# Level masks of a blockwise triangular inverse: from the matrix on GpSimd to the first product's copy on VectorE

## The reference, cut to what matters

```
a_mat = jnp.where(strict, jnp.einsum('bhnik,bhnjk->bhnij', kb, k) * decay, 0.0)
rhs = jnp.concatenate([v * beta[..., None], kb * jnp.exp(gc)[..., None]], axis=-1)
sol = lax.linalg.triangular_solve(a_mat + jnp.eye(CHUNK, dtype=jnp.float32), rhs,
                                  left_side=True, lower=True, unit_diagonal=True)
```

## Time and profile before

| what | value |
| --- | --- |
| median of 3 runs, lowest, highest | 2103.43, 2102.64, 2104.16 us |
| profiled execution: its time, its span | 2101.1 us, 2099.4 us |
| TensorE matmul, busy share of the span | 84% |
| VectorE, ScalarE, GpSimd | 62%, 46%, 10% |
| mixer, first layer | from 291 to some 547 us |
| mixer, second layer | from 1332 to some 1578 us |
| mean granted TensorE clock | 0.923 of full speed |

### The profile page before, as it was taken

How to read it: one execution, slowest core, us unless ns; L and a number is a source line. 1 busy time by engine, 2 the same in 40 slices (tenths; PEclk the granted TensorE clock), 3 DMA queues, 4 the chain that set the end, 5 groups by cost and what they waited for, 6 DMA issues and landing times. The chain is left out here.

```text
span 2099.4 us, 38037 instructions
## 1 busy us (share of the span) xinstructions
PE 1760.4 (84%) x14245; PEld 1412.2 (67%) x14246; DVE 1294.8 (62%) x1877; ACT 958.4 (46%) x1486; POOL 211.8 (10%) x267
## 2 busy tenths in 40 slices
PE   5499978999698399999954999899987939999991
PEld 0299767888444188888843997788873538888881
DVE  0439635666443488696646495576662469999664
ACT  0134533343311288686633445343332238888641
POOL 0000022222000000000010000222220010000002
PEclk8699999999798599999986999999997969999995
DMA  9532043000557499798833220000004069999744
GB/s 393 238 110 79 5 147 128 3 2 2 172 218 274 192 387 399 283 392 339 300 144 111 87 83 1 13 12 2 3 2 143 31 228 389 407 397 397 311 171 180
DMA packets 96326, 376.48 MB, mean 179 GB/s; under 512 B 14478, under 2 KB 35030, under 8 KB 65478
## 3 DMA queue, kind: packets, MB, share of 16 engines
q1 hardware_dynamic: 80486, 316.76, 40.2%
q0 software_dynamic: 8496, 30.94, 3.9%
q10 hardware_dynamic: 7216, 26.97, 3.2%
HBM read 332.86 MB, written 41.78 MB: 178 GB/s over the span
## 5 line engine op out<-in xcount | busy, mean ns | idle before, releaser
L1926 DVE TENSOR_TENSOR expert_w_lo<-shared,expert_w_hi 128x2048 fp32r<-128x2048 f32 x192 | 430.5, 2284 | 44.0 <-ACT expert_w_hi L1868 42.9
L1868 ACT ACTIVATE expert_w_hi<-shared 128x2048 fp32r<-128x2048 f32 x192 | 361.3, 1916 | 56.2 <-PEq L142 52.0
L1810 PE MATMUL ps<-expert_w_hi,expert_x_hi 128*128 128x512 f32 x592 | 232.6, 393 | 5.1 <-DVE expert_x_lo L1922 5.1
L1812 PE MATMUL ps<-expert_w_hi,expert_x_lo 128*128 128x512 f32 x592 | 232.4, 393 | 0.0
L1811 PE MATMUL ps<-expert_w_lo,expert_x_hi 128*128 128x512 f32 x592 | 232.2, 392 | 0.0
L1810 PEld LDWEIGHTS ps<-expert_w_hi,expert_x_hi 128*128 128x128 f32 x592 | 112.4, 190 | 29.4 <-issue 5.9
L1811 PEld LDWEIGHTS ps<-expert_w_lo,expert_x_hi 128*128 128x128 f32 x592 | 112.3, 190 | 23.5
L1812 PEld LDWEIGHTS ps<-expert_w_hi,expert_x_lo 128*128 128x128 f32 x592 | 112.3, 190 | 23.5
L1846 PE MATMUL ps<-expert_w_hi,expert_hid_hi 128*128 128x512 f32 x296 | 118.6, 401 | 1.2 <-ACT expert_hid_hi L1900 0.5
L1847 PE MATMUL ps<-expert_w_lo,expert_hid_hi 128*128 128x512 f32 x296 | 115.6, 391 | 0.0
L964 POOL TENSOR_TENSOR mixer_NTb<-mixer_Bt,consts_sb 128x256 f32<-128x256 f32 x120 | 89.2, 767 | 229.2 <-DVE mixer_Bt L1234 181.1
(11 more groups left out here) (344 smaller groups left out, 3710.7 us busy)
## 6 DMA issues: line engine op xcount, KB each, us to landing
shared<-in_w_gate SPq DMA_DIRECT2D x64, 1024.0 KB, 6.8
shared<-in_w_up SPq DMA_DIRECT2D x64, 1024.0 KB, 8.6
shared<-in_w_down SPq DMA_DIRECT2D x64, 1024.0 KB, 18.8
setup_m_ada_ring<-in_w_ada SPq DMA_DIRECT2D x24, 1024.0 KB, 10.6
shared<-in_w_in SPq DMA_DIRECT2D x10, 2048.0 KB, 8.0
y_table<-expert_y ACTq DMA_DIRECT2D x37, 512.0 KB, 8.8
y_table<-zero SPq DMA_DIRECT2D x1, 12800.0 KB, 41.1
qkv<-in_w_ada SPq DMA_DIRECT2D x11, 1024.0 KB, 5.1
```

What stands on the lines that cost most here:

```text
L1810: pe.matmul(bank, hi, w_hi[:, j, w], start=first, stop=False)
L1812: return pe.matmul(bank, lo, w_hi[:, j, w], start=False, stop=last)
L1868: act.activation(w_hi[:, j, :], raw[:, j, :], ACT.Copy).then_inc(w_hi_done, 1)
L1926: dve.tensor_tensor(w_lo[:, j, :], raw[:, j, :], w_hi[:, j, :].bitcast(F32), ALU.subtract).then_inc(w_lo_done, 1)
```

## The change

The masks of the five levels are no longer multiplied into the matrix. The first product of every level takes the whole `Bt`, and the mask is multiplied into its result, while that is copied from PSUM to `T1`. X is block diagonal at this point, so a block of the result depends on the same block of the matrix alone, and the transposed mask (`level..._{1 - d}`) on the result gives the same `T1`. The copy was an ACTIVATE on ScalarE and is now a tensor_tensor on VectorE (L1234 of the new file). The `level1` mask stays on GpSimd, in a tensor of its own, `N1`.

```
--- before.py
+++ after.py
@@ -903,13 +903,13 @@
         Y = ph.sb("Y", [P, 2, DH, HB])
         T1 = ph.sb("T1", [P, 2, DH, HB])
         T1L = ph.sb("T1L", [P, DH, HB])
-        NTb = ph.sb("NTb", [P, 2, 2, DH, HB])
+        N1 = ph.sb("N1", [P, 2, DH, HB])
         sinks, nsinks = ph.sb("sink", [P, NH]), ph.sb("nsink", [P, NH])
         sink, nsink = (a[:, :].rearrange("p (g j) -> p j g", g=NKV) for a in (sinks, nsinks))
         vctx = ph.sb("vctx", [P, ATT_KV])
         mx, nm, sx, es, rsum, rden = (ph.sb(n, [P, NKV]) for n in ("mx", "nm", "sx", "es", "rsum", "rden"))
         names = ("chain par_in s_in s_zero yf_zero s_out r_p g_p kq_p x0_p t1_p xx_p yy_p t1l_p yl_p ks_p xz_p qs_p qku_p ds_p "
-                 "e_done b_done bl_done n1_done nt_done y0_done qk_done x0_done t1_done x_done y_done yf_done t1l_done yo_done "
+                 "e_done b_done bl_done n1_done y0_done qk_done x0_done t1_done x_done y_done yf_done t1l_done yo_done "
                  "z_done u2_done w_done oz_done o2_done sg_done st_done o_done "
                  "sc_p stats exp_done norm_done pt_p pt_taken pv_p out_done").split()
         s_ = {n: ph.sem(n) for n in names}
@@ -960,21 +960,11 @@
                 pool.memset(S[:, 0], 0.0).then_inc(s_["s_zero"], 1)
                 pool.memset(YF[:, :, :, :], 0.0).then_inc(s_["yf_zero"], 1)
 
-                def masked(slot, d, level):
-                    return pool.tensor_tensor(NTb[:, slot, d], Bt[:, d], row(G.c(f"level{level}_{d}"), DH), ALU.mult)
-
                 for s in range(NT):
                     tt, st = tiles(s), 0 if s == 0 else 1
                     for d in range(2):
                         pool.wait_ge(s_["b_done"], at(s, d))
-                        masked(1, d, 1).then_inc(s_["n1_done"], 1)
-                    for v in range(LV):
-                        for d in range(2):
-                            if v == 1:
-                                pool.wait_ge(s_["y0_done"], at(s, d))
-                            if v >= 2:
-                                pool.wait_ge(s_["t1_p"], lev(s, v - 2, d))
-                            masked(v % 2, d, LEVELS[v]).then_inc(s_["nt_done"], 1)
+                        pool.tensor_tensor(N1[:, d], Bt[:, d], row(G.c(f"level1_{d}"), DH), ALU.mult).then_inc(s_["n1_done"], 1)
                     for d in range(2):
                         if s == 0:
                             pool.wait_ge(s_["s_zero"], 1)
@@ -1079,12 +1069,11 @@
                         eight(d, 0, lambda h: Y[:, d, h, :], lambda h: G.c("eye"), "x0_p")
                     for v in range(LV):
                         for d in range(2):
-                            pe.wait_ge(s_["nt_done"], lev(s, v, d))
                             if v == 0:
                                 pe.wait_ge(s_["x0_done"], at(s, d))
                             else:
                                 pe.wait_ge(s_["x_done"], lev(s, v - 1, d))
-                            eight(d, 0, lambda h: NTb[:, v % 2, d, h, :], lambda h: X[:, d, h, :], "t1_p")
+                            eight(d, 0, lambda h: Bt[:, d, h, :], lambda h: X[:, d, h, :], "t1_p")
                         if v == 2:
                             turn(n0)
                         if v == 3:
@@ -1167,9 +1156,6 @@
                         act.wait_ge(s_["x0_p"], at(s, d))
                         act.activation(flat(X[:, d]), G.ps[:, d, 0:256], ACT.Copy).then_inc(s_["x0_done"], 1)
                     for v in range(LV):
-                        for d in range(2):
-                            act.wait_ge(s_["t1_p"], lev(s, v, d))
-                            act.activation(flat(T1[:, d]), G.ps[:, d, 0:256], ACT.Copy).then_inc(s_["t1_done"], 1)
                         if v == 0:
                             exps(n0)
                         if v == 2:
@@ -1237,12 +1223,15 @@
                                           ALU.mult).then_inc(s_["bl_done"], 1)
                     for d in range(2):
                         dve.wait_ge(s_["n1_done"], at(s, d))
-                        dve.tensor_tensor(Y[:, d], NTb[:, 1, d], row(G.c("eye"), DH), ALU.add).then_inc(s_["y0_done"], 1)
+                        dve.tensor_tensor(Y[:, d], N1[:, d], row(G.c("eye"), DH), ALU.add).then_inc(s_["y0_done"], 1)
                     for d in range(2):
                         dve.wait_ge(s_["kq_p"], at(s, d))
                         dve.tensor_tensor(QK[:, d], bank(2 + d), E[:, d], ALU.mult).then_inc(s_["qk_done"], 1)
                     stats(n0)
                     for v in range(LV):
+                        for d in range(2):
+                            dve.wait_ge(s_["t1_p"], lev(s, v, d))
+                            dve.tensor_tensor(T1[:, d], blocks(d), row(G.c(f"level{LEVELS[v]}_{1 - d}"), DH), ALU.mult).then_inc(s_["t1_done"], 1)
                         for d in range(2):
                             dve.wait_ge(s_["xx_p"], lev(s, v, d))
                             if v == 0:
```

## The result

The changed kernel takes 2105.94 us, the median of 20 runs, beside 2103.4 of the kernel before in 20 runs of its own. The ratio of the means is 1.0016 with a 95% interval from 1.0009 to 1.0023, so it is slower, by 3.4 us (1.9 to 4.8); the medians differ by 2.5. The forecast was 2111.0, in a range from 2105.5 to 2114.5: the direction was right, the size about twice too large, and "slower by over 0.2%", which the prediction gave a chance of 0.80, did not come.

What follows compares the result with a forecast made beforehand. The matrix engine was taken to set the pace in levels without attention work. 4.31 us in the second layer and 3.28 in the first gave 7.6 slower, 2103.4 + 7.6 = 2111.0, range 2105.5 to 2114.5.

Steps and rivals of the forecast that it cites:

- The copy, level 4: Copy to T1 on VectorE: 422 ns instead of 384, so 0.04 us more where the matrix engine waits for it.
- Level 8, the gain of 0.77: Without GpSimd's masks the normalisation pair takes 0.88 us instead of 1.65, so attention's transposes start 0.77 earlier.
- Level 32, the loss of 1.46: Copies wait for attention's statistics on VectorE; the second X starts at 1453.40 instead of 1451.94, 1.46 us lost.
- then 0.04: Level 32: after `sx` ends (0.16 long), 0.04 us pass before the copy of 0.42 starts on VectorE.
- Step 0 was forecast at 1.03: Second layer, step 0: 0.73 + 0.04 - 0.69 + 0.95, together 1.03 us slower.
- Step 1: 0.97: Second layer, step 1: 0.24 + 0.04 - 0.77 + 1.46, together 0.97 us slower.
- The scaling beside the start of Y, 0.33: Level 2: GpSimd's 1096 ns scaling replaces a 767 ns mask, so that Y ends 0.33 us later; bounds 0 and 0.69.
- First layer, step 0, counted at nothing: Matrix engine gaps of 2.73 and 2.26 us swallow a shift of 0.7 or 1.0, so no loss was counted.
- The cover: First layer, step 0: the matrix engine's gaps hide the change's loss; without them it costs 1.0 us more.
- the partial recovery: Rival, level 32: slack behind it returns some 0.8 of 1.46 us, for 2104 to 2107 us; chance 0.12.
- the faster case: Rival: level 8's 0.77 stays and level 32's wait is recovered whole, 0.69 a step, for 2096.5 us; chance 0.04.
- The costly copies: Rival: copies at 830 ns instead of 422 lose 0.41 more at levels 2, 4 and 32, 2123 us; chance 0.05.

Runs made afterwards that it cites:

- masks early: The kernel before with four slots for the masked matrix instead of two, so no GpSimd mask waits for level 8; 2095.4 us, ratio 0.9960.
- scaling late: The changed kernel with GpSimd's scaling of the state held back until level 8's transposes are done; 2104.12 us in one execution.
- copy moved only: The kernel before with T1 as a plain copy on VectorE, all masks left on GpSimd; 2115.99 us, ratio 1.0056.
- Fill in pieces: The kernel before with the first layer's 12.8 MB fill in 25 pieces of 512 KB, five per mixer step; 2093.39 us, ratio 0.9953.
- last level back: The changed kernel with level 32's mask back in the matrix on GpSimd and its copy back on ScalarE; 2097.15 us, ratio 0.9969 to the kernel before.
- copy before statistics: The changed kernel with the second query group's statistics behind level 32's copies on VectorE; 2105.76 us, ratio 1.0012 to the kernel before.

## Why the prediction was right in direction and off in size

- **The copy, level 4:** right. 421 ns where 422 were counted; the second products of level 4 start 0.48 us behind the copy's start, where it was 0.44.
- **Level 8, the gain of 0.77:** right. The pair takes 0.88, and masks early shows the gain alone.
- **Level 32, the loss of 1.46:** the mechanism right, the term 0.12 too large; 1.34 was measured. The step that failed is "then 0.04" between the end of `sx` and the copy. The copy starts 0.08 after `sx` starts, 0.08 before it ends. The earlier trace rows had it: X, which waits for nothing there, starts at 1450.73 behind `sx` of 1450.65.
- **The same 0.12 at every place where the copy queues:** also level 8 and level 2 in step 0, and level 2 in step 1. Step 0 was forecast at 1.03; 1.03 less three times 0.12 is 0.67, and 0.66 was measured. Step 1: 0.97 less twice 0.12 is 0.73, measured 0.68.
- **A saving that the prediction did not have:** the change takes away the matrix engine's second wait ahead of level 2's first product, 0.09 in steps 2 to 4. 0.77 - 0.12 - 0.09 = 0.56, measured 0.57, 0.56 and 0.56.
- **The scaling beside the start of Y, 0.33:** right in size. The pair takes 1.89 instead of the 1.58 that 830 and the trace give, 0.31 more, and the end of the statistics (`sx`) starts 0.3 later in steps 0 and 1 of the second layer. The Trainium skill (SBUF — State Buffer, Who interferes with whom) would have made it 0.69, with the second to issue standing still for the first's whole instruction. Here the wait was shorter than that: in step 2 the second start of Y begins 0.24 behind the scaling and ends 0.28 behind its end, where a full wait would leave 0.42. And GpSimd's own instruction grew too: 1220 ns, where scaling late has 1.04 us for it alone.
- **First layer, step 0, counted at nothing:** it was 0.70 shorter, but that is within what it varies by, and its clock fell. The cover is real: copy moved only loses 2.30 in this step of the second layer and 0.01 here, at full clock in both kernels, and its gaps are 7.0 us in place of 8.6. Fill in pieces shows that the gaps are the fill's.
- **First layer, step 4:** 0.21 longer in place of 0.56, and under the 0.4 that the prediction set as a bound for a full step. There the kernel before has 0.35 that the changed one has not: its first X at level 32 starts 0.43 behind `sx` instead of 0.08, with 0.27 of idle time that no wait ends (the row below). The same row of the second layer has none.
- **Rivals:** the partial recovery and the faster case fall with last level back and copy moved only, which give the loss in full. The costly copies fall with 421 ns.

```profile
519.95 0.16 DVE L1216 TENSOR_TENSOR mixer_sx<-mixer_nm,mixer_sink 128x2 f32<-128x2 f32 x1
520.38 0.42 DVE L1252 TENSOR_TENSOR mixer_X<-mixer_X,ps 128x256 f32<-128x256 f32 x1 [0.27 <-issue]
```

The sum of the corrected terms is 3.1 for the second layer and 2.4 for steps 1 to 4 of the first, 5.5 instead of 7.6, beside 3.0 and 2.0 in the traces. Less the 0.35 of step 4 and the 0.70 of step 0 it is 4.4, as in the traces and inside the 1.9 to 4.8 of the runs, whose middle is 3.4. Why the first layer's step 0 comes out shorter stays open, and so does whether step 4's 0.35 is there in every run.

That the time fell inside the stated range is luck in part. The sum was 4.2 us above the measured 3.4, and the range reached down to 2105.5 for the sake of a rival, the recovery behind level 32, that did not come true.

## What to carry to other kernels

Ask of an operation that changes its engine what it will stand behind in the new queue: here the dearer copy cost some 0.09 us a step, and the statistics ahead of it cost 1.34 us in eight of ten steps. A gain that comes with a move may have a cheaper source: two more buffer slots gave the whole 0.77 at level 8 without moving anything. And where two instructions of VectorE do not depend on each other, count the second from the first one's start in a row of the trace, not from its end plus a gap.

## What the runs showed of the hardware that I had not expected

- A VectorE instruction that does not depend on the one before it starts some 0.08 us before that one's end: the copy, which reads PSUM (1458.73 behind 1458.65 and 0.16), and the second start of Y, which reads SBUF (two of a mean of 984 ns in 1.89 us). Where each reads what the last wrote, there are 0.04 between.
- A second semaphore wait at a matrix product costs 0.09 us, even when it was met long ago, if the product comes right behind the X that it needs; behind an X that is 0.76 us old it cost nothing.
- One transfer of 12.8 MB makes the matrix engine stand still for 1.4 to 2.7 us at a time, 8.6 us in four gaps, with nothing that it waits for in the profile; in 25 pieces of 512 KB, spread over five steps, the same bytes cost under 2 us. The gaps stand some 256 instructions of the matrix engine apart.
- In copy before statistics the matrix engine's clock fell to 1.2 GHz for some 3.5 us behind an idle time of 1.66 to 1.74 us, in three of the five full steps that have so long a one ahead of L1093, and each fall cost 1.5 us or more. In the changed kernel an idle time of 1.65 at another place of the same steps was not followed by one. A saving of 0.4 us a step can be lost again in this way, so the granted clock belongs beside each comparison of steps.
